# A two-block transformer kernel on one core: the first tiles' modulation moved to TensorE, and four product groups opened together

## The chip, the cores and the metric

The kernel runs on one core of a Trainium2 chip. The metric is the device time of one execution in microseconds (us); lower is better. Every engine has its own instruction stream. TensorE (PE) multiplies, VectorE (DVE), ScalarE (ACT) and GpSimd (POOL) work elementwise, SyncE (SP) issues DMAs. The program orders them by semaphores that it sets and waits on by hand.

## What is computed

Two blocks of two layers each on 512 tokens of width 1024, in float32. Only the beginning of the first block matters here:

```python
c_act = jax.nn.silu(c)
for l in range(DEPTH):
    mod = c_act @ mod_w[l] + mod_b[l]
    sh1, sc1, g1, sh2, sc2, g2, sh3, sc3, g3 = jnp.split(mod, N_MOD, axis=-1)
    f = swiglu(modulate(x, sh1, sc1), ffn_in[l, 0], ffn_out[l, 0])
```

`modulate(x, shift, scale)` is `x * (1 + scale) + shift`, and `swiglu` multiplies by a 1024 x 5632 matrix, whose gate and up halves are interleaved here by 128 columns. So before the first product 2 x 1024 numbers (shift and scale of layer 0) must come out of a 1024 x 2048 part of `mod_w`, each a dot product of length 1024 with `silu(c)`.

## The kernel before

The features lie on the 128 partitions, in 8 tiles of 128 features, and the tokens on the free axis (512). A product group is one output tile of 128 features: 8 contraction tiles k, and for each three matmuls (lines 632 to 634). The weights and the activations are each split into a high part (rounded by ACT to the format of fast products, `fp32r`) and a low part (the rest), and a group adds hi*hi, hi*lo and lo*hi: 24 matmuls of 128 x 512.

The weights come as slabs of 128 x 1024 (512 KB) through a ring of three raw buffers: SP loads one (line 514) once the slab three before it has been split, ACT makes the high half (line 548), and DVE or POOL the low half (line 558). For the first layer's first product five buffers hold split slabs. `Lin.ahead` says how far the splitting runs ahead of the group in work (at group 0, up to slab 4), and `Lin.loads` how far the loads do (three more).

Beside that, DVE makes the other modulation rows: 176 of them, one per product group. A row is 128 outputs as dot products of a 128 x 1024 tile with `silu(c)`, broadcast to all partitions (`cb`), in one multiply-and-sum of VectorE (lines 571, 579). SP loads them into a ring of three.

Each engine's stream is a generator, and `weave` runs the generators against each other only to find out the semaphore values; the order in each stream is the one that is written. The beginning consists of the `*_prologue` functions:

- SP (`sp_prologue`): `c` broadcast to `cb`, `cols` (all vectors), then for t = 0 to 7 one 1 MB DMA with the shift and the scale tile t (line 705). The tokens come in two DMAs of 1 MB (line 710), at t = 0 and t = 3, and slabs 0 to 2 at t = 1.
- ACT (`act_prologue`): issues three DMAs of its own (line 713 to 715, 2.6 MB), takes silu of the three `c` vectors, then per tile the high half `UH` of the modulated tokens (line 723) and `ALPHA * x` (line 726). After tile 2 it splits slabs 0 to 2.
- DVE (`dve_prologue`): per tile two dot products (line 746), `1 + scale` (line 750), the modulated tokens in full (line 756), and the low halves of slabs 0 to 2 after tile 2. Then some 25 instructions of 128 x 8 for a vector of a later stage (lines 762 to 782), which begin with a wait for ACT's Exp (line 733).
- POOL (`pool_prologue`): the low half `UL` (line 788).
- PE has no prologue: `pe_ffn` starts with group 0, whose tile k waits for `UL` of tile k.

Then `pe_ffn`, `act_ffn`, `dve_ffn`, `pool_ffn` and `sp_ffn` go through the groups m = 0, 1, 2, ... In DVE's stream group m is: low halves up to `ahead(m)`, the epilogue (for odd m the product of gate and up, line 869), one modulation row (line 571). In SP's it is: slab loads up to `loads(m)`, then the rows.

Of the kernel before, what the change touches and what calls it, by code (L numbers as in the profile page):

```python
# [6 lines left out]
F32 = mybir.dt.float32  # L7
# [242 lines left out]
def rows_in(name):  # L250
# [7 lines left out]
    "v_setup": ("v_eps", "v_first", "v_c1", "v_lam", "v_splus", "v_coef", "v_gate", "v_gq", "v_ca", "v_pad", "v_cz"),  # L258
# [63 lines left out]
def _build(nc, a, out, ctx):  # L322
# [25 lines left out]
    small = sb("small", 4)  # L348
# [42 lines left out]
    ones, ident, one_col = con("ones"), con("ident"), small[:, 2:3]  # L391
# [11 lines left out]
    first = [ar(F0 + 2 * D * t, F0 + 2 * D * (t + 1)) for t in range(8)]  # L403
# [130 lines left out]
    def act_slabs(upto):  # L534
        while to_split["a"][0] <= min(upto, len(SLABS) - 1):
# [10 lines left out]
            if s.slot in (3, 4) and s.lin.name == ("gu", 0, 0, 0):  # L546
                se.wait_ge(*(yield "v_first", 15))
# [12 lines left out]
    def dve_rows(n):  # L560
        for _ in range(n):
# [7 lines left out]
            ve.wait_ge(*(yield "v_row", j - 1) if j else (yield "v_first", 15))  # L569
# [129 lines left out]

    def sp_prologue():  # L700
        sy.dma_start(cb, a["c"].to_broadcast([128, D])).then_inc(*dsig("d_cb"))
        sy.dma_start(cols[:, :], a["cols"]).then_inc(*dsig("d_cols"))
        for t in range(8):
            src = a["mod_w"][0, t:72:8][0:2].rearrange("a p n -> p a n")
            sy.dma_start(first[t].rearrange("p (a n) -> p a n", a=2), src).then_inc(*dsig(f"d_first{t}"))
            if t == 1:
                yield from sp_slabs(NRAW - 1)
            if t == 0 or t == 3:
                h = slice(0, 4) if t == 0 else slice(4, 8)
                sy.dma_start(XA[:, h, :], a["xT"][:, h, :]).then_inc(*dsig(f"d_x{t // 3}"))  # L710

    def act_prologue():
        se.dma_start(cb2, a["c_2"].to_broadcast([128, D])).then_inc(*dsig("d_c2"))
        se.dma_start(cc, a["c_ctx_2"].to_broadcast([128, D])).then_inc(*dsig("d_cc"))
        se.dma_start(const[:, :], a["const"]).then_inc(*dsig("d_const"))
        for i, (v, key) in enumerate(((cb, "d_cb"), (cb2, "d_c2"), (cc, "d_cc"))):
            se.wait_ge(*(yield key,))
            se.activation(v, v, ACT.Silu).then_inc(*sig("a_silu", i))
        for t in range(NT):
            if t % 4 == 0:  # L720
                se.wait_ge(*(yield f"d_x{t // 4}",))
# [5 lines left out]
            if t == 2:  # L727
                yield from act_slabs(2)
# [6 lines left out]
    def dve_prologue():  # L735
# [5 lines left out]
        for t in range(NT):  # L741
# [9 lines left out]
            if t % 4 == 0:  # L751
                ve.wait_ge(*(yield f"d_x{t // 4}",))
# [2276 lines left out]
```

## Time and profile before

| | |
|---|---|
| runs | 3993.61, 3997.81, 3997.95 us; median 3997.81 |
| profiled execution: span from the first to the last instruction | 3993.3 us |
| its granted TensorE clock, mean | 0.967 |
| PE busy | 3725.0 us, 93% of the span |
| DVE, ACT, POOL busy | 2205.1, 1491.8, 1074.7 us |
| DMA | 433.90 MB, mean 109 GB/s |

The profiled execution's own time is known by its span alone, which is 0.3 us below the shortest of the three runs and 4.5 us below their median. The span in 40 slices of 100 us each:

```profile
PE   5999999989999999898999889899999989899999
PEclk8999999999999999999999989799999999899999
DMA  7565314245755555412432411102111112113113
```

A digit is the busy share of a slice in tenths, and for PEclk the granted clock in tenths of full speed. The first slice is the only one in which PE is busy for about half of the time only.

### The profile page before, as it was taken

To read this page: it belongs to the slowest core of one execution; us is meant where nothing else is said; L and a number is where in the kernel's file an instruction comes from. 1 tells how busy PE (TensorE), PEld (TensorE's weight loads), DVE (VectorE), ACT (ScalarE), POOL (GpSimd) and SP (SyncE) were. 2 spreads that over 40 slices of the span, in tenths; PEclk is the share of its full clock that TensorE was granted. 3 is DMA by queue.
4 is the path that set the end of the run, shared out by engine and by line. 5 is a ranking of instruction groups with operands and counts; after the bars stand their busy time and mean duration, and the time that the engine had idled before them with its cause. 6 is when DMAs were issued, how large, how long until landed. Compare 5 with 4: busy or idle time off the path is not lost.

```text
span 3993.3 us, 53032 instructions
## 1 busy us (share of the span) xinstructions
PE 3725.0 (93%) x20868; PEld 3094.4 (77%) x20868; DVE 2205.1 (55%) x3743; ACT 1491.8 (37%) x2560; POOL 1074.7 (27%) x715
## 2 busy tenths in 40 slices
PE   5999999989999999898999889899999989899999
PEld 4888868778889888847888867678878877678777
DVE  6555784667667777645532579831155337840442
ACT  3223563344225322444422422342235324353352
POOL 1102203232013201303201412743211333254224
PEclk8999999999999999999999989799999999899999
DMA  7565314245755555412432411102111112113113
GB/s 269 172 199 171 130 61 170 90 137 180 226 179 154 192 183 168 125 37 85 150 91 91 139 39 48 46 30 74 51 40 36 53 56 69 69 43 99 54 41 99
DMA packets 131590, 433.90 MB, mean 109 GB/s; under 512 B 14480, under 2 KB 14608, under 8 KB 130704
## 3 DMA queue, kind: packets, MB, share of 16 engines
q1 hardware_dynamic: 130912, 427.89, 33.0%
q8 instruction: 167, 2.74, 0.3%
q10 hardware_dynamic: 432, 2.62, 0.2%
q14 instruction: 79, 0.65, 0.1%
HBM read 428.36 MB, written 2.10 MB: 108 GB/s over the span
## 4 chain that ended last, share of the span: by engine, by line
PE 77%; DVE 13%; ACT 4%; issue 3%; DMA 1%; POOL 1%; SPq 0%; DVEq 0%; ACTq 0%
PE ps L632 21%; PE ps L633 21%; PE ps L634 21%; DVE cut L2185 4%; PE ps L1879 1%; DVE cut L558 1%; PE ps L1756 1%; PE ps L1840 1%; PE ps L1856 1%; ACT cut L548 1%; PE ps L1862 1%; PE ps L658 1%; PE ps L1844 1%; PE ps L659 1%; PE ps L660 1%
## 5 line engine op out<-in xcount | busy, mean ns | idle before, releaser
L632 PE MATMUL ps<-cut 128*128 128x512 f32 (+1 forms) x5344 | 1908.2, 357 | 149.2 <-DVE cut L558 53.7
L633 PE MATMUL ps<-cut 128*128 128x512 f32 (+1 forms) x5344 | 1871.4, 350 | 0.0
L634 PE MATMUL ps<-cut 128*128 128x512 f32 (+1 forms) x5344 | 1869.3, 350 | 0.0
L632 PEld LDWEIGHTS ps<-cut 128*128 128x128 f32 x5344 | 1030.7, 193 | 317.7 <-issue 98.9
L633 PEld LDWEIGHTS ps<-cut 128*128 128x128 f32 x5344 | 1031.7, 193 | 131.2 <-issue 5.1
L634 PEld LDWEIGHTS ps<-cut 128*128 128x128 f32 x5344 | 1029.9, 193 | 127.7
L558 POOL TENSOR_TENSOR cut<-cut 128x1024 fp32r<-128x1024 f32 (+3 forms) x280 | 605.0, 2165 | 1334.2 <-ACT cut L548 1333.6
L548 ACT ACTIVATE cut<-cut 128x1024 fp32r<-128x1024 f32 (+3 forms) x680 | 632.1, 938 | 773.3 <-PE ps L634 678.6
L558 DVE TENSOR_TENSOR cut<-cut 128x1024 fp32r<-128x1024 f32 (+3 forms) x400 | 483.0, 1210 | 438.5 <-ACT cut L548 438.4
L888 POOL TENSOR_TENSOR cut<-cut 128x512 fp32r<-128x512 f32 (+1 forms) x100 | 147.5, 1475 | 1041.5 <-ACT cut L849 1041.5
L2185 DVE SCALAR_TENSOR_TENSOR cut<-cut,cols 128x512 f32<-128x512 f32 (+1 forms) x330 | 280.2, 849 | 11.7
L571 DVE CUSTOM_DVE_ANT_0 cut<-cut,cols 128x1024 f32<-128x1024 f32 x128 | 171.4, 1339 | 19.8 <-DMA cut<-in_mod_w 18.1
L869 DVE TENSOR_TENSOR cut<-cut,ps 128x512 f32<-128x512 f32 (+1 forms) x100 | 62.1, 621 | 190.3 <-PE ps L634 190.3
L1905 ACT ACTIVATE cut<-cut,st 128x512 f32<-128x512 f32 (+2 forms) x160 | 110.8, 694 | 140.8 <-DVE st L1938 140.8
L842 ACT ACTIVATE cut<-ps 128x512 f32<-128x512 f32 (+1 forms) x100 | 54.4, 544 | 272.5 <-PE ps L634 272.4
L2353 DVE TENSOR_TENSOR cut<-cut,ps 128x512 f32<-128x512 f32 (+1 forms) x48 | 28.0, 597 | 226.9 <-PE ps L634 226.9
L991 POOL TENSOR_TENSOR cut<-cut 128x256 f32<-128x256 f32 x84 | 86.2, 1026 | 202.6 <-DVE cut L920 202.3
L920 DVE SCALAR_TENSOR_TENSOR cut<-ps,deriv,cut 128x256 f32<-128x256 f32 (+1 forms) x144 | 81.4, 567 | 41.7 <-PE ps L634 41.7
L1017 ACT ACTIVATE cut<-cut 128x256 f32<-128x256 f32 x96 | 39.9, 416 | 146.9 <-DVE cut L920 146.9
L2197 POOL TENSOR_SCALAR const<-cut,cols 128x256 f32<-128x256 f32 x90 | 84.8, 942 | 8.6
L1879 PE MATMUL ps<-cut 128*64 128x128 f32 x1216 | 82.8, 279 | 0.0
L579 DVE CUSTOM_DVE_ANT_0 cut<-cut,cols 128x1024 f32<-128x1024 f32 x48 | 79.7, 1661 | 1.7
(303 smaller groups left out, 3464.5 us busy)
## 6 DMA issues: line engine op xcount, KB each, us to landing
cut<-in_ffn_in SPq DMA_DIRECT2D x200, 512.0 KB, 3.9
cut<-in_mod_w SPq DMA_DIRECT2D x128, 512.0 KB, 4.2
cut<-in_ffn_out SPq DMA_DIRECT2D x96, 384.0 KB, 3.3
cut<-in_ffn_out SPq DMA_DIRECT2D x96, 320.0 KB, 3.0
cut<-in_w_ada SPq DMA_DIRECT2D x48, 512.0 KB, 3.4
cut<-in_w_merge SPq DMA_DIRECT2D x48, 512.0 KB, 3.3
cut<-in_even_in SPq DMA_DIRECT2D x36, 512.0 KB, 3.4
cut<-in_proj SPq DMA_DIRECT2D x48, 256.0 KB, 2.6
```

Source lines behind the costliest of these rows:

```text
L548: se.activation(halves(n)[0], raw(n), ACT.Copy).then_inc(*sig("a_hi", n))
L558: engine.tensor_tensor(lo, raw(n), hi.bitcast(F32), ALU.subtract).then_inc(*sig(which + "_lo", n))
L571: ve.tensor_tensor_reduce(junk, w, cb, 1.0, col("mod_b", 72 * l + i), ALU.mult, ALU.add, modc[:, 72 * l + i:72 * l + i + 1]).then_inc(*sig ...
L632: te.matmul(o, hi[:, k - ka, w], xs[0], start=k == 0, stop=False)
L633: te.matmul(o, hi[:, k - ka, w], xs[1], start=False, stop=False)
L634: ins = te.matmul(o, lo[:, k - ka, w], xs[0], start=False, stop=last)
L888: ge.tensor_tensor(HL[:, t, g[0]:g[1]], FTMP[t % 2][:, g[0]:g[1]], HH[:, t, g[0]:g[1]].bitcast(F32), ALU.subtract).then_inc(*sig("g_hl", g ...
L991: ge.tensor_tensor(total, total if m > 1 else XA[:, 0, g[0]:g[1]], XA[:, m, g[0]:g[1]], ALU.add).then_inc(*sig("g_total", tag, part[-1], m))
L1879: ins = te.matmul(PS[b][64 * s:64 * s + 64, 0:128], J["v"][s][k], pbuf[:, s, k * 128:(k + 1) * 128], start=k == 0, stop=k == nv - 1)
L1905: se.activation(x, x, ACT.Exp, bias=stat(i, 1, s), accum_out=stat(i, 2, s)).then_inc(*sig("a_exp", tag, i, s))
L2185: ve.scalar_tensor_tensor(out=o, in0=x, scalar=c, in1=o, op0=ALU.mult, op1=ALU.add).then_inc(*sig("v_tap", l, t, h0, j))
L2197: ge.tensor_scalar(tmp, i, w, None, ALU.mult).then_inc(*sig("g_tmp", l, x, j))
```

## The change

The shift rows are computed by PE: for each tile t, `pe_shift` adds up 8 plain float32 products of a 128 x 128 piece of the shift weights (a new input layout `mod_shift`, contraction on the partitions) with one column of `silu(c)` (`c_col`, 128 x 8, a new 4 KB input). DVE makes the scale rows as before and adds the bias to PE's result. The low half `UL` moves from POOL to DVE. All DMAs of the beginning are on SP, in pieces of 512 KB, tokens two tiles at a time, slab t behind tile t for t = 0 to 3; `const`, `c_2` and `c_ctx_2` come last. Groups 0 to 3 each take a bank of PSUM and take tiles as they come: group m joins at tile m and catches up.

```diff
     def sp_prologue():
+        sy.dma_start(c_col, a["c_col"]).then_inc(*dsig("d_c"))
         sy.dma_start(cb, a["c"].to_broadcast([128, D])).then_inc(*dsig("d_cb"))
         sy.dma_start(cols[:, :], a["cols"]).then_inc(*dsig("d_cols"))
         for t in range(8):
-            src = a["mod_w"][0, t:72:8][0:2].rearrange("a p n -> p a n")
-            sy.dma_start(first[t].rearrange("p (a n) -> p a n", a=2), src).then_inc(*dsig(f"d_first{t}"))
-            if t == 1:
-                yield from sp_slabs(NRAW - 1)
-            if t == 0 or t == 3:
-                h = slice(0, 4) if t == 0 else slice(4, 8)
-                sy.dma_start(XA[:, h, :], a["xT"][:, h, :]).then_inc(*dsig(f"d_x{t // 3}"))
+            sy.dma_start(shift_w[t], a["mod_shift"][t].rearrange("p (k m) -> p k m", k=8)).then_inc(*dsig(f"d_shift{t}"))
+            sy.dma_start(scale_w[t], a["mod_w"][0, 8 + t]).then_inc(*dsig(f"d_scale{t}"))
+            if t % 2 == 0:
+                sy.dma_start(XA[:, t:t + 2, :], a["xT"][:, t:t + 2, :]).then_inc(*dsig(f"d_x{t // 2}"))
+            if t < len(JOIN):
+                yield from sp_slabs(t)
+        sy.dma_start(const[:, :], a["const"]).then_inc(*dsig("d_const"))
+        sy.dma_start(cb2, a["c_2"].to_broadcast([128, D])).then_inc(*dsig("d_c2"))
+        sy.dma_start(cc, a["c_ctx_2"].to_broadcast([128, D])).then_inc(*dsig("d_cc"))
...
+    def pe_shift(t):
+        b = bank["p_mod", t] = yield from pe_take(("v_first", t), len(JOIN) + t % 4)
+        te.wait_ge(*(yield f"d_shift{t}",))
+        if t == 0:
+            te.wait_ge(*(yield "a_silu", "col"))
+        for k in range(8):
+            ins = te.matmul(PS[b][:, 0:1], shift_w[t][:, k, :], c_col[:, k:k + 1], start=k == 0, stop=k == 7)
+        ins.then_inc(*sig("p_mod", t))
+
+    def pe_prologue():
+        gu = ("gu", 0, 0, 0)
+        for m in range(len(JOIN)):
+            bank[gu, m, 0] = yield from pe_take((("a_sil", "v_hid")[m % 2], gu, m))
+        yield from pe_shift(0)
+        for k in range(NT):
+            if k < NT - 1:
+                yield from pe_shift(k + 1)
+            te.wait_ge(*(yield "v_u0", k))
+            for m, k0 in enumerate(JOIN):
+                if k < k0:
+                    continue
+                if k == k0:
+                    yield from pe_weights(m)
+                hi, lo = [tiles(m, v) for v in halves(m)]
+                o = PS[bank[gu, m, 0]][:, :]
+                for kk in range(k + 1) if k == k0 else (k,):
+                    te.matmul(o, hi[:, kk, :], UH[:, kk, :], start=kk == 0, stop=False)
+                    te.matmul(o, hi[:, kk, :], UL[:, kk, :], start=False, stop=False)
+                    ins = te.matmul(o, lo[:, kk, :], UH[:, kk, :], start=False, stop=kk == NT - 1)
+                if k == NT - 1:
+                    ins.then_inc(*sig("p_mm", gu, m))
...
         for t in range(NT):
...
+            ve.wait_ge(*(yield f"d_scale{t}",))
...
+            ve.tensor_tensor_reduce(junk, scale_w[t], cb, 1.0, col("mod_b", 8 + t), ALU.mult, ALU.add,
+                                    modc[:, 8 + t:9 + t]).then_inc(*sig("v_first", 8 + t))
+            ve.wait_ge(*(yield "p_mod", t))
+            ve.tensor_tensor(sh1, PS[bank["p_mod", t]][:, 0:1], col("mod_b", t), ALU.add).then_inc(*sig("v_first", t))
...
             ve.tensor_scalar(TT[t % 2], XA[:, t, :], sc1, sh1, ALU.mult, ALU.add).then_inc(*sig("v_uf", "start", t))
-            if t == 2:
-                yield from low_slabs("v", ve, 2)
+            ve.wait_ge(*(yield "v_uf", "start", t))
+            yield from low(t)
+            if t < len(JOIN):
+                yield from low_slabs("v", ve, t)
```

`low(t)` is the subtraction that makes `UL` of tile t, after a wait for ACT's `UH`; it signals `v_u0`. In `act_prologue` ACT takes silu of `c_col` and of `cb` only, and splits slab t between `UH` and `ALPHA * x` of tile t (t below 4); the silu of `cb2` and `cc` moves behind the first 22 groups. The wait of slabs 3 and 4 for the last dot product (`v_first`, 15) is gone, since the weights of the beginning now lie elsewhere. `pe_ffn` goes on with group 4. The short instructions for the later stage and the code from group 4 on stay as they are.

## Rows read from the trace of the kernel before

**Rows 1.** The page: PE's busy time, and the chain that ended last, by engine
```profile
PE 3725.0 (93%) x20868; PEld 3094.4 (77%) x20868; DVE 2205.1 (55%) x3743; ACT 1491.8 (37%) x2560; POOL 1074.7 (27%) x715
PE 77%; DVE 13%; ACT 4%; issue 3%; DMA 1%; POOL 1%; SPq 0%; DVEq 0%; ACTq 0%
```

**Rows 2.** Windows: stretch, length, PE, PEld, DVE, ACT, POOL busy, PEclk, DMA share, GB/s
```profile
0.00:32.60 32.60, 0.00 (x0) 0.00 (x0) 11.22 (x23) 10.54 (x13) 3.99 (x7) 1.00 0.96 377
32.60:58.60 26.00, 10.73 (x21) 6.15 (x21) 22.38 (x33) 8.23 (x13) 9.34 (x5) 0.64 0.47 187
...
68.00:80.00 12.00, 12.00 (x54) 9.94 (x54) 7.20 (x8) 3.48 (x5) 1.61 (x1) 1.00 0.84 289
```

**Rows 3.** Timeline of DVE: the three dot products that waited for a DMA (start, length)
```profile
14.98 1.28 DVE L746 CUSTOM_DVE_ANT_0 cut<-cut,cols 128x1024 f32<-128x1024 f32 x1 [14.01 <-DMA cut<-in_mod_w]
...
19.82 1.31 DVE L746 CUSTOM_DVE_ANT_0 cut<-cut,cols 128x1024 f32<-128x1024 f32 x1 [1.38 <-DMA cut<-in_mod_w]
...
26.23 1.28 DVE L746 CUSTOM_DVE_ANT_0 cut<-cut,cols 128x1024 f32<-128x1024 f32 x1 [2.98 <-DMA cut<-in_mod_w]
```

**Rows 4.** Timeline: the rest of tile 2, and a dot product of a later tile
```profile
27.55 1.28 DVE L746 CUSTOM_DVE_ANT_0 cut<-cut,cols 128x1024 f32<-128x1024 f32 x1
...
28.88 0.15 DVE L750 TENSOR_SCALAR deriv<-modc 128x1 f32<-128x1 f32 x1
29.07 0.81 ACT L723 ACTIVATE cut<-cut,modc,deriv 128x512 fp32r<-128x512 f32 x1 [5.04 <-DVE deriv L750]
29.14 0.55 DVE L756 TENSOR_SCALAR cut<-cut,deriv,modc 128x512 f32<-128x512 f32 x1
...
39.96 2.16 DVE L746 CUSTOM_DVE_ANT_0 cut<-cut,cols 128x1024 f32<-128x1024 f32 x1
```

**Rows 5.** Groups by line, 0 to 60 us: splitting a slab (busy us, mean ns)
```profile
L558 DVE TENSOR_TENSOR cut<-cut 128x1024 fp32r<-128x1024 f32 x3 | 3.5, 1220 | 1.7 <-ACT cut L548 1.7
L548 ACT ACTIVATE cut<-cut 128x1024 fp32r<-128x1024 f32 x4 | 4.0, 1040 | 0.0
```

**Rows 6.** Timeline of DVE: from the last tile's tokens to slab 5's low half
```profile
56.51 0.55 DVE L756 TENSOR_SCALAR cut<-cut,deriv,modc 128x512 f32<-128x512 f32 x1
59.42 0.17 DVE L762 TENSOR_SCALAR deriv<-deriv 128x8 f32<-128x8 f32 x1 [2.37 <-ACT deriv L733]
...
64.19 2.35 DVE L558 TENSOR_TENSOR cut<-cut 128x1024 fp32r<-128x1024 f32 x2
72.80 1.28 DVE L571 CUSTOM_DVE_ANT_0 cut<-cut,cols 128x1024 f32<-128x1024 f32 x1 [6.25 <-DMA cut<-in_mod_w]
...
74.01 1.22 DVE L558 TENSOR_TENSOR cut<-cut 128x1024 fp32r<-128x1024 f32 x1
```

**Rows 7.** Timeline of PE from the last tile on
```profile
58.65 0.79 PE L632 MATMUL ps<-cut 128*128 128x512 f32 x1 [3.15 <-POOL cut L788]
59.24 0.63 PE L633 MATMUL ps<-cut 128*128 128x512 f32 x1
...
63.92 0.39 PE L632 MATMUL ps<-cut 128*128 128x512 f32 x1
...
78.24 0.39 PE L632 MATMUL ps<-cut 128*128 128x512 f32 x1
...
83.68 0.39 PE L632 MATMUL ps<-cut 128*128 128x512 f32 x1
```

**Rows 8.** Windows with the columns of rows 2: first products, and three stretches of narrow products
```profile
32.00:37.00 5.00, 4.13 (x9) 2.81 (x9) 4.82 (x6) 1.24 (x2) 0.00 (x0) 1.00 1.02 409
...
691.90:698.70 6.80, 5.49 (x25) 4.77 (x26) 3.16 (x7) 2.34 (x4) 1.92 (x3) 0.50 0.00 0
704.80:710.10 5.30, 5.30 (x49) 5.27 (x48) 3.52 (x6) 3.24 (x6) 0.00 (x0) 1.00 0.07 26
2549.00:2569.00 20.00, 15.27 (x67) 10.19 (x68) 19.22 (x51) 5.85 (x17) 18.18 (x21) 0.50 0.00 1
```

**Rows 9.** Timeline of PE: plain float32 products at the low clock
```profile
694.09 1.91 PE L1394 MATMUL ps<-cut 128*128 128x128 f32 x8
695.94 3.37 PE L1401 MATMUL ps<-cut 64*128 64x256 f32 x14
```

More of the change, by code:

```diff
@@ L402, in _build @@
     F0 = 31232
-    first = [ar(F0 + 2 * D * t, F0 + 2 * D * (t + 1)) for t in range(8)]
+    SHIFT_AT = [F0 + 2 * D * t for t in range(7)] + [E3]
+    SCALE_AT = [F0 + 2 * D * t + D for t in range(6)] + [E3 + D, E3 + 2 * D]
+    shift_w = [ar(o, o + D).rearrange("p (k m) -> p k m", k=8) for o in SHIFT_AT]
+    scale_w = [ar(o, o + D) for o in SCALE_AT]
     HH, HL = rregion(F0, 11, 512)
@@ L703, in sp_prologue @@
         for t in range(8):
[L704 to L718 removed]
+            sy.dma_start(shift_w[t], a["mod_shift"][t].rearrange("p (k m) -> p k m", k=8)).then_inc(*dsig(f"d_shift{t}"))
[7 more added lines that the diff above has]
+        sy.dma_start(cc, a["c_ctx_2"].to_broadcast([128, D])).then_inc(*dsig("d_cc"))
+    def act_prologue():
+        se.wait_ge(*(yield "d_c",))
+        se.activation(c_col, c_col, ACT.Silu).then_inc(*sig("a_silu", "col"))
+        se.wait_ge(*(yield "d_cb",))
+        se.activation(cb, cb, ACT.Silu).then_inc(*sig("a_silu", 0))
         for t in range(NT):
[L720 to L721 removed]
+            if t % 2 == 0:
+                se.wait_ge(*(yield f"d_x{t // 2}",))
             se.wait_ge(*(yield "v_c1", t))
@@ L733, in act_prologue, with act_contexts @@
         se.activation(e, e, ACT.Exp, scale=-1.0).then_inc(*sig("a_lam", 1))
+    def act_contexts():
+        for i, (v, key) in enumerate(((cb2, "d_c2"), (cc, "d_cc"))):
+            se.wait_ge(*(yield key,))
+            se.activation(v, v, ACT.Silu).then_inc(*sig("a_silu", 1 + i))
+    def pe_shift(t):
[28 more added lines that the diff above has]
+                    ins.then_inc(*sig("p_mm", gu, m))
     def dve_prologue():
@@ L782, in dve_prologue @@
         ve.tensor_scalar(sp_, q, 4.0, None, ALU.mult).then_inc(*sig("v_splus"))
-    def pool_prologue():
-        for t in range(NT):
-            ge.wait_ge(*(yield "a_uh", "start", t))
-            ge.wait_ge(*(yield "v_uf", "start", t))
-            ge.tensor_tensor(UL[:, t, :], TT[t % 2], UH[:, t, :].bitcast(F32), ALU.subtract).then_inc(*sig("g_u", "start", t))
-            if t == 2:
-                yield from low_slabs("g", ge, 2)
     def u_ready(u, h):
         def ready(k, gi):
-            return [("g_u", u, k)] if u == "start" else [("v_ul", u, h, k)]
+            return [("v_ul", u, h, k)]
         return ready
@@ L816, in pe_ffn @@
             for i, (gu, tile0, g) in enumerate(ffn_parts(l, f, half)):
-                ready = none if half or i == 2 else u_ready(u, gu[-1])
+                begun = len(JOIN) if gu == ("gu", 0, 0, 0) else 0
+                ready = none if half or i == 2 or begun else u_ready(u, gu[-1])
                 after = (lambda m: pe_ln(u, "B") if m == 0 else nothing(m)) if gu[-1] == "A" else None
-                yield from pe_linear(gu, urhs, [g], lambda m, gi: (("a_sil", "v_hid")[m % 2], gu, m), ready, after)
+                yield from pe_linear(gu, urhs, [g], lambda m, gi: (("a_sil", "v_hid")[m % 2], gu, m), ready, after,
+                                     ms=range(begun, LIN[gu].groups))
             ready = lambda k, gi: [hl_of(l, f, half, k)]
@@ L853, in act_ffn @@
             if half == 0:
+                if (l, f) == (0, 0):
+                    yield from act_contexts()
                 yield from act_linear(("fo", l, f, half), nothing)
@@ L2768, in tensor_program @@
     def tensor_program():
+        yield from pe_prologue()
         yield from pe_ffn(0, 0, "start", 0, "f00", (0, 1))
```

37 lines of the change are left out of this document (18 added, 19 removed).

## The prediction

> **What bounds the kernel now.** I read the page first, then windows, then the timelines of DVE and PE up to 90 us. The page shows PE busy for 93% of the span and the chain on it for 77% [rows 1]: whatever is taken away ahead of the first product group that PE can run without a pause moves the whole rest of the kernel. The windows show where that point lies [rows 2]: no product up to 32.6 us, 21 of them in the next 26.0 us, and from 68 us on PE is busy without a gap. Groups follow each other from 58.65 us, 24 products in 83.68 - 78.24 = 5.44 us, or 0.227 us each [rows 7]. What holds PE up to there is first the DMAs, which are 96% busy [rows 2] and for which DVE waits at tiles 0 to 2 [rows 3], and then DVE itself with two dot products per tile. A dot product takes 1.28 us, and 2.16 us in a stretch where POOL makes `UL` beside it [rows 4].
>
> The yardstick for all that follows is the start of group 5. Before it is at 83.68 us [rows 7], the clock is high, and nothing waits. If PE in the new kernel also runs from group 5 on without a pause, the difference of the two starts is the change in the total.
>
> **Data.** DVE's waits date three landings [rows 3]. By 14.98 us SP's `cb` and `cols` (0.87 MB), tile 0 (1.05) and ACT's three DMAs (2.62) had come: 4.54 MB. By 19.82 and 26.23 us it was 6.64 and 9.26 MB. That is 3.9 us + MB / 0.410. The new order on SP gives by it: shift tile 0 at 7.3 us, scale 0 at 8.6, slab 0 at 11.1, shift 1 at 12.4, scale 1 at 13.7, slab 1 at 15.0, slab 3 at 23.9, and the last scale tile (13.45 MB) at 36.7. SP holds the load of slab 3 until slab 0's low half is there (14.5 us below), and everything behind it waits. I cost this at nothing: ahead of it 7.7 MB are queued, of which 4.3 have landed at 14.5 us, so 8 us of transfers are left to run. `const`, `c_2` and `c_ctx_2` land at about 43 us and have no reader for hundreds of us, nor have the two moved silus.
>
> **DVE and ACT per tile.** The dot product to the next instruction takes 28.88 - 27.55 = 1.33 us. The bias add from PSUM and `1 + scale` are two of 0.15 to 0.2 us; `UH` starts 0.19 us after the latter and takes 0.81 [rows 4]. So the tokens' instruction (line 756) starts 0.55 us after PE's result at the earliest, or after the dot product plus 0.4. No row has the low half of 128 x 512 on DVE; it lies between 0.55 us, for one input [rows 4], and 1.22 us, for twice the length [rows 5]. I take 0.65, half of the latter. For t below 4 ACT's split (1.04) and DVE's (1.22) follow [rows 5]. A tile then costs DVE 4.75 us for t below 4, and 3.3 us after that.
>
> **PE's new work.** Each `pe_shift` is 8 plain float32 products, which the trace shows as two passes each. The nearest rows are passes of 64 to 128 columns with the same 128 x 128 weights. At the high clock 49 took 5.30 us, 0.108 each [rows 8]; at the low clock 8 took 695.94 - 694.09 = 1.85 us, 0.231 each [rows 9]. With one column they may cost less, but the weights must be loaded all the same. I take the row of each clock: 16 passes are 1.7 us high and 3.7 us low. A 128 x 512 product is 0.227 us high, and (63.92 - 59.24) / 11 = 0.425 low [rows 7].
>
> These products are not beside the path: PE's stream is shift(k + 1), then tile k, and DVE's tile k + 1 waits for shift(k + 1). The tiles bring 3, 9, 15, 21 and then four times 12 products.
>
> **The clock.** PE begins slow: nine products took 4.13 us in the first stretch [rows 8], and twelve ran slow from 58.65 us until the rate doubled at 63.92 [rows 7]. So I let the clock stay low until 11 products of tile 2 have run, the first run of 15. After that it meets only narrow passes of 1.7 us between runs of 2.7 us and more. Rows speak both ways here. In 704.8 to 710.1 us nothing but narrow passes ran, densely, at a granted clock of 1.00; in 2549 to 2569 us narrow products with waits between them ran at 0.50 though PE was busy for 15.27 of 20.00 us [rows 8]. The new stage has no waits once it is slow (each shift finds its data), so I take the first. The Trainium skill (TensorE: Matmul & The Clock Gate, section "HAM oscillation — how this bites in real kernels") speaks against it: short bursts between pauses lose the high clock at each tile. By that rule the sum would be that of the second rival below.
>
> **The sum.** Shift 0 runs 7.3 to 11.0; tokens of tile 0 at 11.6, slab 0's low half at 14.5. Shift 1 runs 12.4 to 16.1, tile 0 to 17.4, shift 2 to 21.1, tile 1 (9 slow) to 24.9, shift 3 to 28.6, tile 2 (11 x 0.425 + 4 x 0.227 = 5.6) to 34.2. From here high: shift 4 to 35.9, tile 3 (21) to 40.7, shift 5 to 42.4, tile 4 (12) to 45.1, shift 6 to 46.8, tile 5 to 49.5, shift 7 to 51.2. The tokens' last instruction on DVE starts at 51.8 us (before: 56.51), and the four groups end at 56.6, where before group 4 starts at 78.24 [rows 7].
>
> But group 4 can't follow at once. Its slab's low half stands behind the short instructions in DVE's stream. Before, from the last tokens to the first slab it was 64.19 - 56.51 = 7.7 us [rows 6], covered by groups 0 to 3. Now that cover is spent: 51.8 + 7.7 + 1.2 (one slab, not two) = 60.7. PE stands for 4.1 us and group 4 starts with the low clock: 12 x 0.425 + 12 x 0.227 = 7.8, to 68.5. Slab 5 stands behind modulation row 0, whose load SP issues behind slab 7, which waits for slab 4's low half. That took 72.80 - 66.54 = 6.3 us, then the row and the slab 2.4 [rows 6]. So group 5 starts at 60.7 + 8.8 = 69.5, against 83.68: **14.2 us less**. Beyond it DVE needs 3.2 us a slab in catching up, PE 5.44, so nothing is late.
>
> The profiled execution's span, 3993.3, becomes 3979.1. The median lies 4.5 us above that span, so the sum is 3983.6. Anything within 0.2% (8 us) is no change that could be told.
>
> **Rivals.**
> - *PE is fast at once, or the narrow passes are nearly free.* Then DVE sets the pace: slab 3's low half at 14.5 + 3 x 4.75 = 28.7, four runs and three shifts up to tokens 7 give 44.5, and group 5 starts at 62.2: 21.5 less, **3976**. For it: 8 of 16 passes could vanish with one column. Against: nine products at the start ran slow [rows 8].
> - *The clock stays low to the last tile.* Tile 2 then ends at 35.0, and shift 3.7, tile 3 of 9.0 and tiles of 5.1 us bring tokens 7 to 69.6 and group 5 to 87.3: 3.6 more, **4001**, which is no change. For it: the 20 us at 0.50 [rows 8]. Against: twelve slow products in a row were enough at 58.65 [rows 7], and tile 3 has 21. A clock that falls once or twice gives about 3990.
> - *A narrow pass costs as much as a slow full one*, 0.425 us, and the clock stays low. It sits between the tiles, on PE: a shift is 6.8 us, tokens 7 come at about 93, group 5 at 111: 27 more, **4025**. From 0.27 us a pass at the low clock on, the kernel is slower by over 8 us. For it: no row has one column. Against: passes of 128 columns took 0.231 [rows 9].
> - *The smaller DMAs are slow.* The Trainium skill (DMA: Bandwidth & Descriptors, section "Rules for kernel authors") asks for 1 MiB or more per DMA; now they are 512 KB. The last scale tile lands at 36.7 and is wanted at about 48, so the rate may fall to 0.31 MB/us at no cost. The stretch from 32 us, with the last 1 MB tiles and slabs of 512 KB in it, ran at 409 GB/s [rows 8]. I give it no chance of its own.
>
> **How the numbers follow.** Forecast 60%; fast at once 18%; low clock to the end 15% (half of it near 3990 to 3995); dear passes 5%; 2% for the rest. The likeliest gives 3983.6. Its own bounds: 9 to 15 slow products (1.2 us either way), low half 0.55 to 1.22 (hidden behind PE), the add from PSUM up to 0.55 (3 us more), and 2 us of spread between runs: 3979 to 3989. The range takes in the fast rival and the falling clock: 3974 to 3993. Faster by over 0.2% has the forecast, the fast rival and a part of the third: 0.83; same 0.12; slower 0.05.
>
> **What would show it.** Narrow products at 3.7 us per tile up to about 28 us and 1.7 after; tile 3's 21 products at 0.227 us; DVE idle in the prologue until PE; a PE wait of some 4 us for DVE's low half (line 558) ahead of group 4; a DVE wait of 6 us for row 0; group 5 starting at 69 to 70 us. I am wrong if the clock is 0.50 beyond 36 us, if a pass costs more than 0.25 us, or if PE waits again after group 5.

## The result, and the profile after

The changed kernel takes 3977.81 us, the median of 4 runs (3974.16 to 3979.82), against 3995.71 (4 runs) for the kernel before on the same chips: a ratio of 0.9962, with 0.9951 to 0.9974 as its interval. That is 0.38% less, beyond the 0.2% that can be told apart. The profiled execution took 3979.66 us, its span 3978.4 where it was 3993.3: 14.9 us less, against 14.2 forecast. The median was forecast at 3983.6 us, and came out 5.8 us lower.

The page of the profile of the changed kernel: busy times, and the chain by engine, as [rows 1].

```profile
PE 3738.8 (94%) x20996; PEld 3112.3 (78%) x20996; DVE 2195.4 (55%) x3743; ACT 1492.0 (38%) x2561; POOL 1060.1 (27%) x707
...
PE 77%; DVE 13%; ACT 4%; issue 3%; DMA 1%; POOL 1%; SPq 0%; DVEq 0%; ACTq 0%; POOLq 0%
```

PE has 128 passes more, the 8 x 16 of the shift rows, and is busy for 13.8 us more in a shorter span. The windows of the beginning, with the columns of [rows 2]:

```profile
8.20:33.50 25.30, 23.72 (x87) 21.49 (x88) 17.20 (x30) 9.12 (x12) 0.00 (x0) 1.00 1.03 409
33.50:57.50 24.00, 24.00 (x138) 20.67 (x136) 11.55 (x34) 8.99 (x13) 0.00 (x0) 1.00 0.55 227
...
61.60:70.00 8.40, 8.40 (x25) 6.64 (x26) 3.73 (x5) 0.67 (x2) 0.00 (x0) 0.64 0.84 300
```

PE, which had no product before 32.66 us, now works from 8.2 us on and without a pause from 33.5 to 57.5. (PEclk reads 1.00 up to 33.5 us, although the products there are slow; the trace has no record of the clock so early. Take the rate from the products.) PE's timeline shows each step of the forecast:

```profile
8.24 3.57 PE L750 MATMUL ps<-small,cut 128*128 128x1 f32 x16 [8.24 <-DMA cut<-in_mod_shift]
13.35 3.57 PE L750 MATMUL ps<-small,cut 128*128 128x1 f32 x16 [1.53 <-DMA cut<-in_mod_shift]
16.79 0.77 PE L770 MATMUL ps<-cut 128*128 128x512 f32 x1
...
18.21 3.41 PE L750 MATMUL ps<-small,cut 128*128 128x1 f32 x16
21.48 0.77 PE L770 MATMUL ps<-cut 128*128 128x512 f32 x1
...
33.14 0.58 PE L771 MATMUL ps<-cut 128*128 128x512 f32 x1
33.56 0.39 PE L772 MATMUL ps<-cut 128*128 128x512 f32 x1
...
34.48 1.84 PE L750 MATMUL ps<-small,cut 128*128 128x1 f32 x16
36.19 0.48 PE L770 MATMUL ps<-cut 128*128 128x512 f32 x1
...
61.59 0.77 PE L633 MATMUL ps<-cut 128*128 128x512 f32 x1 [3.97 <-DVE cut L559]
...
67.69 0.39 PE L635 MATMUL ps<-cut 128*128 128x512 f32 x1
...
69.99 0.39 PE L633 MATMUL ps<-cut 128*128 128x512 f32 x1
```

A shift is 3.4 to 3.6 us up to tile 2 and 1.84 after it. The products double their rate at 33.5 us, within tile 2. Then PE stands for 3.97 us ahead of group 4 (61.59), loses the high clock, has it again at 67.7, and begins group 5 at 69.99. On DVE's timeline stand what it waits for in the beginning, the last tokens, and the stretch that PE waits for:

```profile
28.91 0.16 DVE L795 TENSOR_TENSOR modc<-ps,cols 128x1 f32<-128x1 f32 x1 [2.59 <-PE ps L750]
...
52.55 0.55 DVE L803 TENSOR_SCALAR cut<-cut,deriv,modc 128x512 f32<-128x512 f32 x1
53.40 0.69 DVE L785 TENSOR_TENSOR cut<-cut 128x512 fp32r<-128x512 f32 x1 [0.30 <-ACT cut L727]
55.47 0.17 DVE L811 TENSOR_SCALAR deriv<-deriv 128x8 f32<-128x8 f32 x1 [1.38 <-ACT deriv L737]
...
60.23 1.22 DVE L559 TENSOR_TENSOR cut<-cut 128x1024 fp32r<-128x1024 f32 x1
66.27 1.28 DVE L572 CUSTOM_DVE_ANT_0 cut<-cut,cols 128x1024 f32<-128x1024 f32 x1 [4.82 <-DMA cut<-in_mod_w]
```

The start of group 5, 83.68 us in [rows 7], is 13.7 us earlier; after it PE waits for nothing up to 200 us. The remaining 1.2 us of the 14.9 come later, where the code is the same, and they are not to be read as an effect. ACT's table loads mark the same places in both programs: that of 395.1 us comes 13.7 us earlier, that of 893.5 comes 19.5 earlier, that of 1902.6 comes 23.3, that of 3584.2 comes 15.0. So the lead of the start is whole at 395 us, and behind that the rest of the kernel drifts by several us between two executions. The experiments come back to this.

### The profile page after: what moved, and what is told of

Read it like the earlier page. It is cut to its first block, busy times and chain, and to the rows that moved or that the text cites. A ratio compares the mean times of both kernels' runs of the same rounds, so it can differ in the third digit from the quotient of the medians.

```text
span 3978.4 us, 53300 instructions
## 1 busy us (share of the span) xinstructions
PE 3738.8 (94%) x20996; PEld 3112.3 (78%) x20996; DVE 2195.4 (55%) x3743; ACT 1492.0 (38%) x2561; POOL 1060.1 (27%) x707
## 3 DMA queue, kind: packets, MB, share of 16 engines
q1 hardware_dynamic: 131904, 430.52, 33.5%
## 4 chain that ended last, share of the span: by engine, by line
PE 77%; DVE 13%; ACT 4%; issue 3%; DMA 1%; POOL 1%; SPq 0%; DVEq 0%; ACTq 0%; POOLq 0%
PE ps L633 21%; PE ps L634 21%; PE ps L635 21%; DVE cut L2229 4%; PE ps L1923 1%; DVE cut L559 1%; PE ps L1800 1%; PE ps L1900 1%; PE ps L1884 1%; ACT cut L549 1%; PE ps L1906 1%; PE ps L1888 1%; PE ps L631 1%; PE ps L659 1%; PE ps L661 1%
```

## Experiments

Theory: the start of group 5 sets the gain, and the start is a chain on PE and DVE whose terms are the shift products, the clock, the short instructions on DVE and group 4 at the low clock. Rivals: the gain comes from another part of the change (one group or four, the loads' order), or DVE or the DMAs set the pace. Each edit is made on the changed kernel. Where only one run is given, its total stands for little, and the profile is what is read. The runs were made on several chips; each total is compared with the kernel before on the same chip.

**One group in place of four.** The slabs come by tile all the same, but only group 0 takes tiles as they come; groups 1 to 3 follow it.

```
-    JOIN = [0, 1, 2, 3]
+    JOIN = [0]
```

> Only group 0 takes tiles as they come; groups 1 to 3 run whole behind it. All else as in the changed kernel (group 4 starts at 61.6 us there, group 5 at 70.0). Theory (group 5 starts at the later of two chains, PE's products and DVE's way from the last tokens over the short instructions to slabs 4 and 5): PE has only 3 wide products between two shifts, so the tokens' last instruction comes earlier, at about 46 us, group 0 ends near 48, groups 1 to 3 take 12 x 0.427 + 60 x 0.227 = 18.7 us behind it, group 4 starts near 67 without a wait and group 5 near 72.3: 2.3 us later than in the changed kernel. Rival (the four groups under the arriving tiles are the whole gain): group 5 near 83, as before the change.

Measured: 3982.09 us (10 runs; the kernel before 3992.0 in 15), ratio 0.9972 (0.9962 to 0.9983). PE's timeline:

```profile
46.99 0.80 PE L770 MATMUL ps<-cut 128*128 128x512 f32 x1 [0.59 <-DVE cut L785]
...
51.85 0.44 PE L635 MATMUL ps<-cut 128*128 128x512 f32 x1
...
71.87 0.39 PE L633 MATMUL ps<-cut 128*128 128x512 f32 x1
```

Group 5 begins at 71.87 us, 0.4 from the 72.3 expected and far from the rival's 83, and only 1.9 us later than in the changed kernel's first profile. Two effects nearly cancel. PE has only three wide products per tile now, so the last tokens come 7.1 us earlier on DVE's timeline, although the clock stays low up to 51.9 us:

```profile
45.41 0.55 DVE L803 TENSOR_SCALAR cut<-cut,deriv,modc 128x512 f32<-128x512 f32 x1
```

But 72 products are left for after the last tile, and from the last tokens to group 5 it takes 26.5 us, where the changed kernel takes 17.4. A part of these 72 runs in the time in which PE would wait for group 4's low half, and group 4 runs at the high clock. So the four groups shorten the way behind the last tile by 9 us and lengthen the tiles by 7.

**Both rows on the vector engine.** `pe_shift` goes; DVE makes the shift row by a second dot product per tile.

```
-            ve.wait_ge(*(yield "p_mod", t))
-            ve.tensor_tensor(sh1, PS[bank["p_mod", t]][:, 0:1], col("mod_b", t), ALU.add).then_inc(*sig("v_first", t))
+            ve.wait_ge(*(yield f"d_shift{t}",))
+            ve.wait_ge(*(yield "v_first", 8 + t))
+            ve.tensor_tensor_reduce(junk, shift_w[t].rearrange("p k m -> p (k m)"), cb, 1.0, col("mod_b", t), ALU.mult, ALU.add,
+                                    modc[:, t:t + 1]).then_inc(*sig("v_first", t))
```

> PE makes no shift products; DVE makes both rows of a tile as before the change; four groups, DMA order and DVE's low half as changed. Theory: DVE alone sets the pace, 5.9 us per tile up to tile 3 and 4.5 us after, so the last tokens come at about 49.7 us (52.6 in the changed kernel), group 4 at 58.7, group 5 at 67.1: 2.9 us earlier than in the changed kernel. So the shift rows on PE cost more than they save. Rival (moving the rows off DVE is what brings the gain): the last tokens at 58 us or later and group 5 at 75 us or later.

Measured: 3974.04 us (6 runs), ratio 0.9958 (0.9945 to 0.9971); group 5 at 66.06. The last tokens on DVE:

```profile
49.65 0.55 DVE L802 TENSOR_SCALAR cut<-cut,deriv,modc 128x512 f32<-128x512 f32 x1
```

The waits of this kernel in its first 92 us:

```profile
PE ps L767 <- DVE cut L559: 15.6, 1, 15.6
...
PE ps L767 <- DVE cut L782: 10.5, 6, 2.8
```

Now PE waits for DVE, and the start is still no later than with the rows on PE. With four groups under the tiles, the products that the change adds on PE save nothing at group 5. Against the first profile of the changed kernel they cost 3.9 us; how much of that is the clock, the repetition of the changed kernel below shows.

**Each shift's products twice.**

```
-        for k in range(8):
+        for k in list(range(8)) * 2:
```

> Each shift row is computed twice (the second time over the first, same result): 16 more narrow passes per tile and nothing else. Theory (the passes stand on the path at 0.21 us low and 0.107 high): shifts 0 and 1 add 5.4 us (1.5 of 6.9 fall into the wait for shift tile 1), 2 and 3 add 3.4 each, 4 to 7 add 1.7 each: group 5 starts at 70.0 + 19 = 89. Rival (narrow passes lower the clock): 3.4 us of them at a stretch bring the clock back to 0.50 in the tiles behind, and group 5 starts at 98 or later. Other rival (passes hide beside DVE): less than 8 us more.

Measured: 4002.29 us (one run), with group 5 at 89.62 us. PE's timeline:

```profile
33.76 3.86 PE L750 MATMUL ps<-small,cut 128*128 128x1 f32 x32
37.48 0.63 PE L770 MATMUL ps<-cut 128*128 128x512 f32 x1
...
41.21 0.40 PE L770 MATMUL ps<-cut 128*128 128x512 f32 x1
...
42.60 3.63 PE L750 MATMUL ps<-small,cut 128*128 128x1 f32 x32
```

The shift products are on the path: with them doubled group 5 comes 19.6 us later. Tile 0 starts 4.9 us later (21.67 for 16.79; 1.5 of the first two shifts' 6.9 fall into a wait), the third shift costs 3.4 and five at the high clock 1.7 each, together 16.8. The other 2.8 are left for the clock, net of the 1.5 us by which PE's wait ahead of group 4 is shorter (2.45 us, not 3.97). The clock rose at 34.2 us, fell in the 3.86 us of narrow passes (the products behind them, at 37.48, are slow), rose at 41.2, fell again at 54.7, right behind another 3.62 us of them, and twice more behind the next two such stretches, though not behind those at 42.6. In none of the traces did the changed kernel's 1.7 us between runs of 12 and more cost the high clock. So the prediction's second rival is not far off: with narrow stretches twice as long it came true in part. The expectation's 89 was hit with a different sum, since it had no falling clock.

**The three late loads back on ACT's queue.**

```
     def act_prologue():
+        se.dma_start(cb2, a["c_2"].to_broadcast([128, D])).then_inc(*dsig("d_c2"))
+        se.dma_start(cc, a["c_ctx_2"].to_broadcast([128, D])).then_inc(*dsig("d_cc"))
+        se.dma_start(const[:, :], a["const"]).then_inc(*dsig("d_const"))
```

> const, c_2 and c_ctx_2 (2.6 MB) go back to ACT's queue at the start. Theory: they share the DMA engines with the first tiles, so shift tile 1 lands at about 3.9 + 6.1 / 0.41 = 18.8 us, not 13.3, and PE's chain, group 4 and group 5 come 5 to 5.5 us later (group 5 at 75.2). Rival (the start waits for PE's and DVE's work, the data were there anyway): under 1 us.

Measured: 3986.7 us (one run), with group 5 at 70.52. PE's timeline:

```profile
14.09 3.57 PE L750 MATMUL ps<-small,cut 128*128 128x1 f32 x16 [14.09 <-DMA cut<-in_mod_shift]
...
22.64 0.77 PE L770 MATMUL ps<-cut 128*128 128x512 f32 x1
...
30.36 0.40 PE L771 MATMUL ps<-cut 128*128 128x512 f32 x1
```

and on DVE's the dot product of tile 2:

```profile
26.14 1.28 DVE L792 CUSTOM_DVE_ANT_0 cut<-cut,cols 128x1024 f32<-128x1024 f32 x1
```

The first shift tile lands at 14.09 instead of 8.24 us: the 2.6 MB on the other queue delay it by 5.85. The Trainium skill (DMA: Bandwidth & Descriptors, section "Issuing engines are not separate DMA queues") says that DMAs of all issuing engines interleave on the same 16 engines, and this agrees. Tile 2's dot product is back at 26.14 us, where it was before the change (26.23, [rows 3]) and not at 20.27. So the move of these three loads brings the whole lead of the data; the smaller pieces and the new order make tile 2 start no earlier (two slabs have been split by then, though, and before the change none).

The expected 75.2 us for group 5 was missed by 4.7 against the first profile: the first tile's products come 5.85 us later (22.64 against 16.79), yet the clock rises at 30.2 us, in tile 1, and no longer at 33.5, in tile 2, so 0.5 us of the delay is left. In the repetition of the changed kernel below the clock also rises in tile 1, and group 5 starts at 65.49. Against that one the loads cost 5.0 us at group 5, as expected.

**The short instructions behind the first 22 groups.** DVE's lines 808 to 831 and ACT's `Abs` and `Exp`, made for a later stage, move to where their reader is near.

```
+    def dve_lam():
         e, s, s2, p, q = [deriv[:, 104 + 8 * i:112 + 8 * i] for i in range(5)]
...
+                if (l, f) == (0, 0):
+                    yield from dve_lam()
```

> The short instructions for the later stage (DVE's 28 of 128 x 8 and ACT's Abs and Exp with their table loads) move behind the first 22 groups; all else as in the changed kernel. Theory (they are the first wait behind the four groups): slab 4's low half is there at 56.1 us, before PE ends the four groups at 57.5, so group 4 follows at once with the high clock and ends at 62.9; then row 0, 7.2 us from slab 4's low half to slab 5's, holds group 5 to 63.4: 6.6 us earlier than 70.0, and as much in the total. Rival (the instructions stall PE as much where they now stand): group 5 at 63.4, but under 3 us in the total, with a PE wait of over 3 us at the start of the product with the ffn_out weights, near 160 us.

Measured: 3971.91 us (4 runs; the kernel before 3988.91 in 11), ratio 0.9961 (0.9946 to 0.9975). On DVE's timeline slab 4's low half starts at 55.07 us instead of 60.23, and the wait for the row is longer:

```profile
61.98 1.28 DVE L572 CUSTOM_DVE_ANT_0 cut<-cut,cols 128x1024 f32<-128x1024 f32 x1 [5.69 <-DMA cut<-in_mod_w]
```

PE goes on into group 4 without a wait, at 57.74 and at the high clock, where 57.5 was expected. Group 5 starts at 64.56, 5.4 us earlier than in the changed kernel, but 1.2 behind the expectation, and PE's timeline has the reason:

```profile
64.56 0.47 PE L633 MATMUL ps<-cut 128*128 128x512 f32 x1 [1.22 <-DVE cut L559]
```

With the short instructions gone the next wait is for slab 5 behind row 0. The short instructions cost 4 us of waiting and the low clock of group 4 after it; 1.2 us of that comes back as this new wait. The clock rose at 34.2 us here, close to the first profile's 33.5, so the two starts compare. The rival, that the instructions stall PE as much where they now stand, is out: PE waits for nothing more up to 200 us. In the total the gain is 17.0 us over the kernel before, and the changed kernel's was 17.9 and, repeated, 9.2: the runs do not show the 5.4 us by themselves.

**Row 0's load earlier.** SP loads the first three modulation rows ahead of `const`.

```
+        yield from sp_rows(MRING - 1)
         sy.dma_start(const[:, :], a["const"]).then_inc(*dsig("d_const"))
```

> Modulation rows 0 to 2 are loaded ahead of const in the beginning; the short instructions stay. Theory (in the changed kernel row 0's wait of 4.8 us lies beside group 4, which runs slow to 70.0): DVE has slab 5 at about 64 us instead of 68.7, and group 5 still starts at 70.0, within 0.5. Rival (row 0 is what sets group 5, as my prediction had it at 69.5): group 5 starts 3 us or more earlier.

Measured: 3979.57 us (one run). DVE's timeline:

```profile
61.27 1.28 DVE L572 CUSTOM_DVE_ANT_0 cut<-cut,cols 128x1024 f32<-128x1024 f32 x1
```

DVE's wait of 4.8 us is gone: the row's dot product starts 5.0 us earlier, and slab 5's low half follows it at once. Group 5 starts at 69.92, as before the edit. The wait for row 0 costs nothing here: PE is slow in group 4 and is the later of the two. It costs 1.2 us where group 4 is fast throughout, as in the run above, and 0.1 to 0.3 us in four other runs, whose group 4 had less of the low clock (rows on vector, loads on ACT, filler, low half on POOL): there PE stands for that long ahead of group 5.

**Products without use, to have the high clock early.** 9 plain float32 products of 128 x 512 on zeros before shift 0, and 5 after it.

```
+        te.wait_ge(*(yield "v_eps", 3))
+        for _ in range(9):
+            te.matmul(PS[7][:, :], TT[2][:, 0:128], TT[2][:, :], start=True, stop=True)
         yield from pe_shift(0)
+        for _ in range(5):
+            te.matmul(PS[7][:, :], TT[2][:, 0:128], TT[2][:, :], start=True, stop=True)
```

> PE runs 9 plain float32 products of 128 x 512 on zeros (18 wide passes) from about 1.5 us and 5 more between shifts 0 and 1, into a bank that nothing reads; they compute nothing. Theory (the low clock up to 33.6 us is a cost of its own): shifts and tiles run fast from the start, slab 3's low half comes at 28.6 us, the last tokens at 44.8 (52.6 in the changed kernel), group 4 at 53.8, group 5 at 62.2: 7.8 us earlier. Rival (waits between the first tiles, or products of zeros, do not keep the clock up): first shift of tile 2 still 3.4 us, group 5 within 2 us of 70.0.

Measured: 3976.14 us (8 runs), ratio 0.9967 (0.9957 to 0.9977); group 5 at 63.78. PE's timeline:

```profile
1.50 9.79 PE L759 MATMUL ps<-cut 128*128 128x512 f32 x18 [1.50 <-DVE small L785]
11.13 1.84 PE L750 MATMUL ps<-small,cut 128*128 128x1 f32 x16
12.83 4.54 PE L762 MATMUL ps<-cut 128*128 128x512 f32 x10
```

The clock is high from 5.2 us on and every shift takes 1.84. The filler was too long: a plain pass of 512 columns took about 0.44 us at the high clock (10 of them from 12.83 to 17.20 us), so shift 0 began 2.9 us late and tile 0 at 18.91. Tile 2 came 3.0 us earlier than in the first profile all the same, and group 5 6.2 earlier; against the repetition of the changed kernel it is 1.7 earlier. The total doesn't show it: 12.8 us less than the kernel before on the same chip, which lies between the 17.9 and the 9.2 of the changed kernel.

**Rows on the vector engine, the short instructions later, row 0 early**, the second, fifth and sixth edit together.

> Both rows of a tile on DVE (as in e2), the short instructions behind the first 22 groups (as in e5), rows 0 to 2 loaded early (as in e6). Theory (the parts add up once both waits behind the four groups are gone): PE ends the four groups at 54.0 us as in e2, slab 4 is there at 53.3 and slab 5 at 55.8, so PE does not wait and group 5 starts at 59.4: 10.6 us earlier than in the changed kernel, total near 3967. Rival (a new wait takes their place, the loads of slabs 6 and 7 or DVE's catching up): group 5 or 6 waits over 2 us and the gain over the changed kernel is under 7 us.

Measured: 3965.77 us (4 runs, 3959.37 to 3970.0), ratio 0.995 (0.9933 to 0.9966). PE's timeline:

```profile
51.33 0.50 PE L770 MATMUL ps<-cut 128*128 128x512 f32 x1 [1.46 <-DVE cut L785]
...
54.20 0.39 PE L633 MATMUL ps<-cut 128*128 128x512 f32 x1
...
59.64 0.39 PE L633 MATMUL ps<-cut 128*128 128x512 f32 x1
```

Groups 4 and 5 start 0.2 us from where they were expected, with nothing between them, and PE waits for nothing from there to 200 us. The clock rose late here, at 32.1 us, and yet the last tokens come as in the run with the rows on DVE alone, whose clock rose at 25.1:

```profile
49.74 0.55 DVE L805 TENSOR_SCALAR cut<-cut,deriv,modc 128x512 f32<-128x512 f32 x1
```

This version has the lowest median of all and beats the kernel before by 23.1 us. Its slowest run (3970.0) is faster than all 13 of the changed kernel (3974.16 and 3973.53 at the least), but on another chip; the intervals of the ratios overlap with that of the first result, so that it beats the changed kernel is likely and not shown. Its group 5 is 10.4 us ahead of the changed kernel's first profile and 5.9 ahead of the second.

**All waits out, with the rows on PE**: a shorter filler (5 and 3 products), the short instructions later, and on SP slabs 4 and 5, rows 0 to 2 and slab 6 ahead of `const`.

> The shift rows stay on PE. Filler products sized by e7's rows (5 before shift 0, 3 between shifts 0 and 1; on zeros, they compute nothing), the short instructions behind the first 22 groups, and on SP slabs 4 and 5, rows 0 to 2 and slab 6 ahead of const, c_2 and c_ctx_2. Theory: the clock is high from about 5 us; tile 3 ends at 32.0, tile 7 at 47.9; slab 4's low half is there at 46.6 and slab 5's at 49.1, so group 4 starts at 47.9 and group 5 at 53.4: 16.6 us earlier than in the changed kernel, 30 us earlier than before the change, ratio 0.9925 to before. With e8 (59.6) it tells that PE's rows are worth having only at the high clock. Rival (the data set the pace now: the last scale tile lands at 36.7 us and slab 4 at 38): a DMA wait over 3 us in the tiles, group 5 at 58 us or later.

Measured: 3970.21 us (4 runs; the kernel before 3989.65 in 12), ratio 0.9951 (0.9934 to 0.9967). PE's timeline:

```profile
14.95 0.48 PE L780 MATMUL ps<-cut 128*128 128x512 f32 x1
...
16.98 3.46 PE L755 MATMUL ps<-small,cut 128*128 128x1 f32 x16 [1.09 <-DMA cut<-in_mod_shift]
20.30 0.77 PE L780 MATMUL ps<-cut 128*128 128x512 f32 x1
```

Group 5 at 57.82 is the earliest of all, but 4.4 us behind the expected 53.4. The clock was high from 6.9 us on and fell at about 17: three short products, a wait of 1.09 us for a shift tile, and the next shift ran slow. It was back at 24.0. The rival had put the delay on the data, with a wait of over 3 us in the tiles: the longest DMA wait there was this one. With the slow shift behind it (1.6 us more) and the slow products of tile 1 (1.8 more) it makes up the 4.4.

**The low half on POOL, and the changed kernel once more**, on one chip. The first has `UL` on POOL, as before the change:

```
-            yield from low(t)
...
+            ge.tensor_tensor(UL[:, t, :], TT[t % 2], UH[:, t, :].bitcast(F32), ALU.subtract).then_inc(*sig("g_u", "start", t))
```

> UL is made by POOL as before the change, all else as changed. Theory (PE's narrow passes set the pace from tile 1 on): POOL's 1.27 us and the slower dot products beside it (2.16 us) fall into DVE's waits for PE of up to 3.3 us, and group 5 starts within 1 us of 70.0. Rival (taking POOL out is part of the gain): group 5 3 us or more later.

> The changed kernel once more, on the chip of e9, as the yardstick. Group 4 starts at 61.6 and group 5 at 70.0, each within 0.7 us, the clock rising in tile 2; the total differs from its last span (3978.4) by a few us, since the runs of one kernel spread by 8 us and more while the start does not.

Measured: 3977.82 us (one run) with POOL (group 5 at 65.11), and 3980.45 (9 runs, 3973.53 to 3986.05) for the changed kernel, ratio 0.9974 (0.9964 to 0.9984), with group 5 at 65.49. PE's timeline of the changed kernel's second profile:

```profile
21.39 0.77 PE L770 MATMUL ps<-cut 128*128 128x512 f32 x1
...
25.25 1.84 PE L750 MATMUL ps<-small,cut 128*128 128x1 f32 x16
26.96 0.48 PE L770 MATMUL ps<-cut 128*128 128x512 f32 x1
```

Moving the low half to DVE made no difference beyond 0.4 us with the shift rows on PE. With both rows on DVE it makes little per tile either: from tile 4 on the tiles' first dot products follow each other at 4.51, 4.48 and 4.91 us before the change, with the low half on POOL, and at 4.54, 4.48 and 4.53 in the run with the rows on DVE. The repetition missed its expectation (70.0 within 0.7): the same program, with its starts within about 0.1 us up to tile 1, had the high clock at 25.1 instead of 33.5, and group 5 4.5 us earlier. The total was no shorter for it (span 3978.2 against 3978.4), and the nine runs' median lies only 9.2 us below the kernel before on that chip, where the four of the first result had 17.9. The kernel before was profiled once only, so how far its own start moves is not known.

This changes how the other profiles are read. Those with the rise in tile 1 are compared with this one. With the rows on DVE group 5 starts at 66.06, here at 65.49. And the two versions differ in what the clock does to them. With the rows on DVE the last tokens come at 49.65 and 49.74 us, with the rise at 25.1 and at 32.1, though in the first of them the clock was low again from 31.9 to 35.3. With the shift rows on PE they come at 52.55 in the first profile and here at

```profile
48.53 0.55 DVE L803 TENSOR_SCALAR cut<-cut,deriv,modc 128x512 f32<-128x512 f32 x1
```

So the shift rows on PE are worth 1 us when the clock rises in tile 1 and cost 3 when it rises in tile 2: their slow passes are on the path.

And it shows what one span can tell. The table splits the span of each profiled execution at group 5:

| kernel | clock up, us | group 5, us | from there to the end, us |
|---|---|---|---|
| before | 63.9 | 83.68 | 3909.6 |
| changed | 33.5 | 69.99 | 3908.4 |
| changed, again | 25.1 | 65.49 | 3912.7 |
| one group | 51.9 | 71.87 | 3912.9 |
| rows on vector | 25.1 | 66.06 | 3905.5 |
| shifts twice | 34.2 | 89.62 | 3911.4 |
| loads on ACT | 30.2 | 70.52 | 3915.0 |
| short later | 34.2 | 64.56 | 3909.5 |
| row 0 early | 33.6 | 69.92 | 3908.4 |
| filler | 5.2 | 63.78 | 3915.2 |
| vector rows, short later | 32.1 | 59.64 | 3898.5 |
| all waits out | 6.9 | 57.82 | 3909.2 |
| low half on POOL | 24.9 | 65.11 | 3911.5 |

(The clock column is the time at which it first rose for a run of products; in some it fell again.) In 12 of the 13 the rest takes 3905.5 to 3915.2 us, whatever the beginning was, and the two profiles of the changed kernel are 4.3 us apart in it; beyond group 5 the kernels differ in nothing but the few short instructions and loads. A gain at group 5 passes to the end, plus or minus 5 us. The version with the lowest time owes some 10 us of its profiled execution to a rest of 3898.5, which no other has. What singled this rest out stays open. Its median lies 23.1 us below the kernel before on its chip, the changed kernel's 17.9 and 9.2 on theirs: 5.2 and 13.9 more, where the starts of group 5 give 10.4 and 5.9. Medians from different chips don't separate the start from the rest.

## Why the prediction was right

**The sum.** The cost, the waits and their order came out as forecast up to group 4; only the last step was on the wrong wait (below). Every landmark of the chain lies within 1 us of its forecast, but the errors don't simply add. Shift 0 landed at 8.24 us (7.3 forecast) and shift 1 at 13.35 (12.4): the straight line through DVE's waits was 0.9 us early. The narrow passes at the low clock took 0.21 to 0.22 us, not 0.231, which gave 0.3 back per shift; at the high clock 16 took 1.7, as forecast. The clock rose after 11 products of tile 2, the last tokens were at 52.55 (51.8), PE's wait was 3.97 us (4.1), group 4 at 61.59 (60.7) and group 5 at 69.99 (69.5). The low half on DVE took 0.69 us against 0.65. The span of 3979.1 us was forecast to 0.7 us. The median was not: the forecast added the 4.5 us by which the median of the kernel before lay above its profiled span, and in the changed kernel the median lies 0.6 us below the span (2.3 above it in the repetition). So the median fell below the forecast's own bounds of 3979 to 3989, and nearer to the 3976 of the first rival, though that rival's cause did not occur.

**The term that was lucky.** That the clock would rise within tile 2 was taken from a run of slow products; the second profile has it rise in tile 1, 8.4 us earlier. The step "I let the clock stay low until 11 products of tile 2 have run" holds for one of two executions. It is an event with a spread, and its price at group 5 is 4.5 us. The bounds of 1.2 us either way were too narrow for it, and the first profile's agreement to 0.5 us is partly chance. The range of the total was wide enough for it.

**The step that failed.** "Slab 5 stands behind modulation row 0 … so group 5 starts at 60.7 + 8.8" put the end of the start on the wrong wait. DVE did wait for row 0 (4.82 us, 6.3 forecast), but slab 5's low half began at 67.48 and was done before 69, and PE finished the slow group 4 only at 69.99. Taking the row's wait away moved group 5 by 0.07 us. PE needed 8.4 us for group 4 and not 7.8, since 14 and not 12 of its products were slow. The two chains were 1.0 us apart in the forecast itself (68.5 against 69.5), so the number held though the cause did not.

**Costs taken as nothing.** SP held the load of slab 3 until 15.35 us, with the DMAs at 409 GB/s from 8.2 to 33.5 us and no wait for a DMA on PE behind shift 1. The loads moved behind the tiles landed with no reader waiting. The smaller DMAs were no slower. The Trainium skill (DMA: Bandwidth & Descriptors, section "Rules for kernel authors") asks for 1 MiB each, and here 512 KB each ran at the 409 GB/s of [rows 8].

**The rivals.** *Fast at once* was wrong in its cause (shifts 0 to 3 ran slow, and 0 to 2 in the repetition), but its start of 62.2 us was near what an early clock gives: with a filler the clock was high from 5.2 us on and group 5 came at 63.78. *Clock low to the end*: in the changed kernel narrow stretches of 1.7 us between runs of 12 or more products never lowered the clock, in either profile. The Trainium skill (TensorE: Matmul & The Clock Gate, section "HAM oscillation — how this bites in real kernels") describes a kernel that loses the high clock at each tile, in the wait for a DMA between short bursts. The prediction's rival counted the narrow passes as such a pause, and the traces don't bear that out: PE was busy through them. But the clock fell with narrow stretches of 3.6 to 3.9 us, with each shift's products twice, and behind three products and a wait of 1.09 us, with all waits out. *Dear narrow passes* is out: 0.107 and 0.21 to 0.22 us.

**Where the gain comes from.** Three stretches, each from a start on a timeline to the next, add up to the start of group 5:

| kernel | tile 2's first dot product, us | from there to the last tokens | from there to group 5 | group 5 |
|---|---|---|---|---|
| before | 26.23 | 30.28 | 27.17 | 83.68 |
| changed | 20.27 | 32.28 | 17.44 | 69.99 |
| changed, again | 20.19 | 28.34 | 16.96 | 65.49 |
| one group | 20.11 | 25.30 | 26.46 | 71.87 |
| rows on vector | 21.25 | 28.40 | 16.41 | 66.06 |
| vector rows, short later | 21.35 | 28.39 | 9.90 | 59.64 |
| loads on ACT | 26.14 | 28.01 | 16.37 | 70.52 |

The changed kernel gains 6.0 us up to tile 2, loses 2.0 in the tiles and gains 9.7 behind the last tokens: 13.7. The first gain is the loads': it goes when they are put back on ACT's queue. The last one is the four groups': with one group it is gone. What it costs in the tiles hangs on the clock: 2.0 us lost in the first profile, 1.9 won in the second.

That TensorE relieves the vector engine is true on DVE, which now idles for PE, as the waits of the changed kernel's first 92 us show:

```profile
DVE modc L795 <- PE ps L750: 12.8, 7, 3.3
```

It is no sure gain at group 5, since DVE with both rows gets there about as early, and the low half's place is worth 0.4 us at most. But each of these was taken out alone, and the parts stand in for each other. With one group, where PE has little to do in a tile, the rows on PE seem to pay: the tokens come at 45.41 us, and DVE with both rows needs until 49.65. An estimate from these two puts group 5 at 71.87 + 4.2 = 76.1 us with neither the four groups nor the rows on PE. No run had both out.

## What to carry to other kernels

Order a kernel's first loads by the time of their first use, and put nothing on another queue that isn't wanted soon: 2.6 MB there cost the first tile 5.85 us and, at like clocks, the start of group 5 5.0. Once a beginning is dense, look for work in it whose reader is far off: moving some two dozen short vector instructions brought group 5 forward by 5.4 us. Opening four groups on arriving tiles took 9 us from behind the last tile and put 7 into the tiles; giving TensorE half of the vector engine's rows beside it was worth 1 us or cost 3, as the clock rose. And before a difference of a few us is believed, take the start and the rest apart and profile the same kernel twice, the one before the change too, for the rest spread by 10 us here, and the clock alone moved the start by 4.5.

## What the runs showed of the hardware that was not expected

The moment at which the clock rises isn't fixed by the program: 33.5 and 25.1 us in two executions whose starts agree within about 0.1 us up to tile 1, behind 23 slow products in one and 12 in the other. In the run with one group, where each tile had three products between shifts of 3.4 us, it stayed low from 16.6 to 51.9 us although PE was hardly ever idle, and rose behind eleven slow wide products in a row. Why it stayed low for so long there stays open. A plain float32 product of 128 x 512 costs two passes of about 0.44 us at the high clock, against the 0.227 us of the products in the groups. And a pass of one column costs 0.107 us at the high clock and 0.21 at the low one, as much as those of 64 to 128 columns in [rows 8] and [rows 9] (0.108 and 0.231): fewer columns bought next to nothing. That it is the loading of the 128 x 128 weights that one pays for is argued, not shown.
